# Pages turned later, square root's table loaded early, constants queued behind the first weights, and the input copied by VectorE, in a two-layer decoder step

## The chip, the cores and the metric

One NeuronCore of a Trainium2 chip runs the whole program in one launch. The metric is device time in microseconds (us), the median of three runs. TensorE (PE) multiplies and transposes, VectorE (DVE) and ScalarE (ACT) work elementwise, GpSimd (POOL) and SyncE (SP) issue DMAs, each engine in the order of its own program. They meet through semaphores.

## What is computed

The reference is one inference step of a two-layer decoder with D_MODEL 1024, on 512 prompt tokens and 8 x 4 sample tokens (544 columns in all). Layer 0 is retention and a gating MLP, with one joint input and one joint output projection. Layer 1 is sparse attention with three branches. Each layer ends with a gated convolution MLP, and every sub-layer stands between two RMS norms:

```python
def rms_norm(x, g):
    y = x * lax.rsqrt(jnp.mean(x * x, -1, keepdims=True) + EPS)
    return y * g
...
y = jnp.concatenate([ret_out, sg_out], axis=-1) @ w_out      # even layer's output projection
xp = xp + rms_norm(mp, norm_mix_post[l])
fp, cp = conv_ffn(rms_norm(xp, norm_ffn_pre[l]), ...)
xp = xp + rms_norm(fp, norm_ffn_post[l])
...
full_c = jnp.concatenate([gather_pages(pool_c, page_table), rows_c], axis=1)
kc, vc = compress(full_c, pe_k, pe_v, phi_k, phi_v)          # layer 1, from 16 cached pages
```

The compressed keys and values of the cached pages need nothing of layer 0, so the kernel makes them during layer 0.

## The kernel before

Activations lie transposed in SBUF: `xT` is 8 blocks (`dc`, `k` or `m`) of 128 features by 544 columns. Every matrix product is made of three products with operands split into a rounded high part and a rest: `hH` and `hL` for activations, `wH` and `wL` for weights.

**Weights** come in 107 units of up to 1 MB. SP loads a unit into one of two slots of `raw` (L505), as soon as the unit two before it has been split. ACT rounds it to `wH` (`split_hi`, L1158 is the line of every ACT operation), and DVE makes `wL` (`split_lo`, L1504). PE waits for that (`unit(u)`). The products go to one of two PSUM slots (`gemm`), by chunks of 128 output features: L582 and L849 for feature chunks, L598 for token chunks.

**A norm** squares the 8 blocks (ACT), sums them in PE (`square_sum`, L611, four matmuls after each square), takes the root (`root`, ACT Sqrt into `rq`), the reciprocal (`rec`, DVE L1510 into `rr`), spreads it over the partitions (`spread_rstd`, PE L618) and multiplies (DVE, `y`, L1522 before a sub-layer, L1532 and L1536 after it). `norm_fill` then makes `hH` (ACT) and `hL` (DVE L1515) block by block, 8 times. A function that is not in ACT's loaded table makes the compiler put a table load in front of it. `Copy`, `Square` and `Identity` never had one.

**The start.** SP issues the identity, the sample input, the prompt input in two DMAs of 1 MB (L500), then the weights. POOL issues `spread` and the four rows of gains (L1934), directly behind them 15 tables of constants for layer 0 (L1944) and two loads of the retention state (L1947). PE transposes the input block by block into two PSUM banks in turn (L557). For each block ACT copies the bank to `xT` and squares it. PE takes the square sum of block `dc - 1` behind the transposes of block `dc`. A bank is used again when its copy is done (`xt_ready`). DVE copies only the sample columns (L1540) and the gains (L1542), then runs `split_lo(0)` and behind it `norm_fill(0)`, which begins with the reciprocal.

**The output projection of layer 0** (`project_out(E_OUT)`, four units of two chunks, k0 to k7) carries the cached pages. I call the two pages of sample b pair p0 to p7. POOL looks up and loads 16 pages of 256 KB (`load_page`, L1970) after the barrier that ends the mixer (`meet`). Each page buffer holds four pages, so a page `n >= 4` waits until `pairs` of two pairs before has been filled. DVE rearranges a pair with two copies (L1721, semaphore `paired`), behind `split_lo` of the unit it stands with: p0 and p1 with the first, and so on. PE transposes it (`turn_pages`, L557, four transposes a page, two PSUM banks) in front of chunks k1 to k7, p7 behind k7. ACT takes each page out with two copies (`take_pages`, `page_ev`). In ACT's program they stand in front of that chunk's own copy, behind `split_hi` of the next unit where the chunk is the first of its unit. Page n is transposed when page n - 2 was taken out.

SP's loads of the phi weights (1 MB in four DMAs) and of the last output unit also start at that barrier. The other roots stand after this projection (`root(1)`), before and after both MLPs (`root(2)` to `root(4)`, `root(6)`, `root(7)`) and after layer 1's output projection (`root(5)`).

## Time and profile before

| | |
|---|---|
| three runs | 1733.72, 1735.07 and 1737.88 us; median 1735.07 us |
| the profiled execution | 1738.51 us, of which 1736.5 us from the first to the last instruction |
| mean granted TensorE clock | 0.952 |
| busy: PE, DVE, ACT, POOL | 92%, 45%, 40%, 13% of the span |
| instructions | 31072 |

All times of the trace count from the first instruction. In a timeline row the columns are start, duration, engine, line, operation, output and input by the program's names, and in brackets the idle time of the engine before it and what ended it. A row xN merges N instructions. In the chain of waits a row says from when, for how long and by what the end of the program was held up. "DMA" there is a transfer that is waited for. PEclk is the granted clock, 1.00 for 2.4 GHz and 0.50 for 1.2 GHz.

### The profile page before, as it was taken

The numbers are of one execution on the slowest core, as the hardware profiler recorded it, in microseconds if no ns is written. First come the engines' busy times: TensorE is split into PE (matmuls) and PEld (weight loads), VectorE is DVE, ScalarE is ACT, GpSimd is POOL, SyncE is SP. The second block draws the span as 40 slices with busy tenths as digits, with TensorE's granted clock in tenths as the row PEclk, the third lists the DMA queues.
The fourth block names the chain that finished last, engine by engine and source line by source line (L and its number), as shares of the span: only waits on it lengthen the run. The fifth ranks groups of instructions, "written<-read, shape, count | busy, mean of one in ns | idle before, by whom it ended". The sixth has DMA issues, their size and how long they took to land.

```text
span 1736.5 us, 31072 instructions
## 1 busy us (share of the span) xinstructions
PE 1603.8 (92%) x12951; PEld 1459.8 (84%) x12951; DVE 780.4 (45%) x1266; ACT 691.7 (40%) x1316; POOL 218.7 (13%) x582
## 2 busy tenths in 40 slices
PE   4999997999999999978999799988969999999996
PEld 2989976789999999967899556556859999999995
DVE  2565452455542555344112465653145553255523
ACT  4123123455542545223322465554335553255422
POOL 3000001200010000001013244432100000000000
PEclk8999998999999999987999898998979999999998
DMA  6122316312333232324333100004312223333231
GB/s 209 49 75 95 100 55 140 90 50 72 89 88 106 73 89 65 97 81 135 117 123 73 43 21 2 1 10 138 82 27 72 74 82 89 93 94 83 66 88 52
DMA packets 185559, 138.46 MB, mean 80 GB/s; under 512 B 11376, under 2 KB 177504, under 8 KB 185392
## 3 DMA queue, kind: packets, MB, share of 16 engines
q1 hardware_dynamic: 175536, 106.31, 21.5%
q0 software_dynamic: 9920, 30.74, 6.1%
q8 instruction: 69, 1.13, 0.3%
q14 instruction: 34, 0.28, 0.0%
HBM read 128.21 MB, written 13.01 MB: 81 GB/s over the span
## 4 chain that ended last, share of the span: by engine, by line
PE 79%; DVE 8%; ACT 5%; DMA 3%; issue 3%; POOLq 1%; POOL 1%; SPq 0%; DVEq 0%; ACTq 0%
PE gemm L849 40%; PE gemm L582 18%; PE gemm L598 9%; PE misc L557 5%; DMA raw<-in_o_w_in 2%; PE gemm L983 2%; PE misc L1014 1%; DVE y L1522 1%; DVE hL L1515 1%; ACT pr L1158 1%; DVE y L1532 1%; DVE pr L1812 1%; POOLq L490 1%; DVE xT L1536 1%; PE misc L618 1%
## 5 line engine op out<-in xcount | busy, mean ns | idle before, releaser
L1504 DVE TENSOR_TENSOR wL<-raw,wH 128x2048 fp32r<-128x2048 f32 (+2 forms) x107 | 222.1, 2075 | 256.3 <-ACT wH L1158 256.3
L849 PE MATMUL gemm<-hH,wH 128*128 128x272 f32 x1280 | 268.4, 291 | 0.0
L849 PE MATMUL gemm<-hH,wL 128*128 128x272 f32 x1280 | 264.9, 288 | 0.0
L849 PE MATMUL gemm<-hL,wH 128*128 128x272 f32 x1280 | 263.9, 288 | 0.0
L1158 ACT ACTIVATE wH<-raw 128x2048 fp32r<-128x2048 f32 (+2 forms) x107 | 185.3, 1732 | 64.1 <-PE gemm L582 32.7
L849 PEld LDWEIGHTS gemm<-hH,wH 128*128 128x128 f32 x1280 | 200.6, 188 | 5.9 <-issue 4.9
L849 PEld LDWEIGHTS gemm<-hL,wH 128*128 128x128 f32 x1280 | 201.1, 189 | 0.0
L849 PEld LDWEIGHTS gemm<-hH,wL 128*128 128x128 f32 x1280 | 199.8, 189 | 0.0
L598 PE MATMUL gemm<-wH,hH 128*128 128x256 f32 x560 | 164.8, 294 | 14.3 <-DVE hL L1515 8.5
L1732 DVE SCALAR_TENSOR_TENSOR conv<-up,rows_t,conv 128x560 f32<-128x560 f32 x88 | 70.5, 802 | 214.3 <-ACT conv L1158 214.3
L598 PE MATMUL gemm<-wL,hH 128*128 128x256 f32 x560 | 162.4, 290 | 0.0
L598 PE MATMUL gemm<-wH,hL 128*128 128x256 f32 x560 | 161.1, 288 | 0.0
L582 PE MATMUL gemm<-hH,wH 128*128 128x272 f32 (+1 forms) x656 | 141.8, 298 | 8.1 <-DVE hL L1515 4.5
L582 PE MATMUL gemm<-hL,wH 128*128 128x272 f32 (+1 forms) x656 | 137.8, 292 | 0.0
L582 PE MATMUL gemm<-hH,wL 128*128 128x272 f32 (+1 forms) x656 | 137.5, 291 | 0.0
L1158 ACT ACTIVATE up<-gemm 128x32 f32<-128x32 f32 (+2 forms) x264 | 66.0, 324 | 176.0 <-PE gemm L849 154.5
L598 PEld LDWEIGHTS gemm<-wH,hH 128*128 128x128 f32 x560 | 109.2, 195 | 19.4 <-DVE hL L1515 7.2
L582 PEld LDWEIGHTS gemm<-hH,wH 128*128 128x128 f32 (+1 forms) x656 | 104.4, 191 | 14.8 <-issue 9.0
L598 PEld LDWEIGHTS gemm<-wH,hL 128*128 128x128 f32 x560 | 110.3, 197 | 0.0
L849 PE MATMUL gemm<-aH,wH 128*128 128x272 f32 x528 | 110.2, 290 | 0.0
L598 PEld LDWEIGHTS gemm<-wL,hH 128*128 128x128 f32 x560 | 109.7, 196 | 0.0
L849 PE MATMUL gemm<-aH,wL 128*128 128x272 f32 x528 | 108.9, 287 | 0.0
(329 smaller groups left out, 2672.9 us busy)
## 6 DMA issues: line engine op xcount, KB each, us to landing
raw<-in_f_w_in SPq DMA_DIRECT2D x88, 512.0 KB, 5.0
raw<-in_f_w_out SPq DMA_DIRECT2D x32, 704.0 KB, 4.6
raw<-in_e_w_in SPq DMA_DIRECT2D x12, 1024.0 KB, 5.1
raw<-in_o_w_in SPq DMA_DIRECT2D x10, 1024.0 KB, 5.2
raw<-in_e_w_out SPq DMA_DIRECT2D x4, 1024.0 KB, 6.7
pages<-in_cache_cmp POOLq DMA_DIRECT2D x16, 256.0 KB, 3.5
raw<-in_o_w_out SPq DMA_DIRECT2D x16, 256.0 KB, 6.1
rows<-in_cache_sel POOLq DMA_DIRECT2D x12, 256.0 KB, 2.9
```

What stands on the lines that cost most here:

```text
L490: page = eng.value_load(a["page_table"][b:b + 1, pg:pg + 1], min_val=0, max_val=N_POOL - 1)
L557: ins = pe.transpose(out, in_, ident[base:base + k, base:base + k])
L582: ins = pe.matmul(gemm[c % 2][0:m, n, 0:TH], w, x[:, k, n * TH:(n + 1) * TH], start=(n_k == 0 and part == 0), stop=(n_k == nk - 1 and part ...
L598: ins = pe.matmul(gemm[c % 2][:, 0, 0:width], x, w, start=(k == 0 and part == 0), stop=(k == DC - 1 and part == 2))
L618: ins = pe.matmul(misc[:, 1 + q // 2, (q % 2) * TQ:(q % 2 + 1) * TQ], spread[:, q, :], rr[:, :], start=True, stop=True)
L849: ins = pe.matmul(gemm[odd][:, n, 0:TH], w, x[:, k, n * TH:(n + 1) * TH], start=(k == 0 and part == 0), stop=(k == nk - 1 and part == 2))
L983: ins = pe.matmul(slot[:, g2, 0:keys], qTs[j][half, r, rows], (ksT, kwT)[br][half, j, 0:keys], start=True, stop=True)
L1014: ins = pe.matmul(misc[64 * g2:64 * g2 + 64, 2 + grp % 2, r * P:(r + 1) * P], kvN[:, 1 + kt, (2 * br + 3) * 256 + g * HD:(2 * br + 3) * 25 ...
L1158: order(act.activation(out, in_, func, **kw), sem_)
L1504: order(dve.tensor_tensor(unit_view(wL, u), unit_view(raw, u), unit_view(wH, u).bitcast(F32), ALU.subtract), lo_ready)
L1515: order(dve.tensor_tensor(hL[:, k, :], src, hH[:, k, :].bitcast(F32), ALU.subtract), h_ready)
L1732: order(dve.scalar_tensor_tensor(conv[:, j, :], U[:, j, 1:1 + CW], w[:, 17:18], conv[:, j, :], ALU.mult, ALU.add))
```

## The change

Five edits in one:

1. `turn_pages` and `take_pages` follow a table `PAGES_AT`: p0 in front of k3, p1 of k4, p2 of k5, p3 and p4 of k6, p5 and p6 of k7, p7 still behind k7. DVE's rearrangement follows `PAIRED_AT`: none with the first unit, p0 and p1 with the second, p2 to p4 with the third, p5 to p7 with the fourth.
2. `load_root` is a Sqrt of a 128x1 tile into a tile that nothing reads. It stands at ACT's very start, in front of the squares of retention's norm, in layer 1's output projection behind the second unit's `split_hi`, and in each MLP behind the first output chunk of its second half.
3. POOL waits for the first weight unit to land before it issues the 15 constants and what follows.
4. DVE instead of ACT copies the 8 input blocks out of PSUM.
5. In the first norm DVE does the reciprocal first and `split_lo(0)` behind it.

```diff
--- before.py
+++ after.py
@@ -209,6 +209,7 @@
         spread = sb("spread_sb", [P, 4, P])
         mean_d, mean_k = sb("mean_d", [P, 32]), sb("mean_k", [P, 32])
         eps, pool_mark = sb("eps", [P, 1]), sb("pool_mark", [1, 1])
+        root_probe = sb("root_probe", [P, 1])
         gains = sb("gains", [P, DC, 8])
         kcs = sb("kcs", [P, DB, 2, NCS])
         vcs = sb("vcs", [2 * NCS, DB, P])
@@ -411,6 +412,8 @@
             if eng is nc.gpsimd:
                 eng.wait_ge(phase, N_BAR * (n + 1))
 
+        PAGES_AT = {3: (0,), 4: (1,), 5: (2,), 6: (3, 4), 7: (5, 6)}
+        PAIRED_AT = ((), (0, 1), (2, 3, 4), (5, 6, 7))
         FILL_AFTER = [0, E_OUT, F0, O_IN, F1]
         NORM_GAIN = [0, 2, 4, 6, 1, 3, 5, 7]
 
@@ -810,8 +813,9 @@
                 for i in range(4):
                     unit(first + i)
                     for j in range(2):
-                        if fill and 2 * i + j:
-                            turn_pages(4 * i + 2 * j - 2)
+                        if fill:
+                            for b in PAGES_AT.get(2 * i + j, ()):
+                                turn_pages(2 * b)
                         feature_chunk(first + i, j, DC, hH, hL, fill if i == j == 0 else None, MIX_FIRST,
                                       part_of=(4 if fill and i == j == 0 else 0, None))
                         if 2 * i + j:
@@ -1193,14 +1197,16 @@
                 act.wait_ge(gemm_done, c + 1)
                 return gemm[c % 2]
 
+            def load_root():
+
+                activate(root_probe[:, :], eps[:, 0:1], ACT.Sqrt)
+
+            act.wait_ge(consts, 3)
+            load_root()
+            act.wait_ge(gain_ready, 1)
             for dc in range(DC):
-                act.wait_ge(xt_turned, dc + 2)
-                activate(xT[:, dc, NS:T], misc[:, 1 + 2 * (dc % 2), :], ACT.Copy, xt_ready)
-                if dc == 0:
-                    act.wait_ge(gain_ready, 1)
                 act.wait_ge(xt_ready, dc + 1)
                 square(0, dc, xT[:, dc, :], sqx)
-            act.wait_ge(gain_ready, 2)
             root(0)
 
             split_hi(0)
@@ -1228,6 +1234,7 @@
                             activate(lns[:, 2, :], lns[:, 1, :], ACT.Sqrt, ln_root, bias=eps[:, 0:1], scale=1.0 / P)
                     elif what in (6, 7):
                         activate(halves(silu_g[:, 2 * (what - 6) + j, :]), chunk_ready(c)[:, :, 0:TH], ACT.Silu, evacuated[c % 2])
+            load_root()
             act.wait_ge(o_ev, 4)
             act.wait_ge(so_ev, 4)
             for h in range(RH):
@@ -1269,9 +1276,12 @@
             def project_out(first, n):
                 for i in range(4):
                     split_hi(first + i + 1)
+                    if first == O_OUT and i == 0:
+                        load_root()
                     for j in range(2):
-                        if first == E_OUT and 2 * i + j:
-                            take_pages(4 * i + 2 * j - 2)
+                        if first == E_OUT:
+                            for b in PAGES_AT.get(2 * i + j, ()):
+                                take_pages(2 * b)
                         c, m = FIRST_CHUNK[first + i] + j, 2 * i + j
                         activate(halves(y[:, m, :]), chunk_ready(c)[:, :, 0:TH], ACT.Copy, evacuated[c % 2])
                         act.wait_ge(evacuated[c % 2], c // 2 + 1)
@@ -1339,6 +1349,8 @@
                             square(n, m, y[:, m, :], sqf)
                         if m == 0:
                             tail_out(e, FH - 1, half, layer)
+                            if half:
+                                load_root()
                 root(n)
 
             def tail_out(e, i, half, layer):
@@ -1516,7 +1528,13 @@
 
             def norm_fill(n, fill):
 
-                rec(n)
+                if n:
+                    rec(n)
+                else:
+                    dve.wait_ge(root_ready, 1)
+                    order(dve.reciprocal(rr[:, :], rq[:, :]), rec_ready)
+                    split_lo(0)
+                    dve.wait_ge(rstd_ready, 1)
                 for k in range(DC + 1):
                     if k < DC:
                         order(dve.scalar_tensor_tensor(halves(y[:, k, :]), halves(xT[:, k, :]), gains[:, k, NORM_GAIN[n]:NORM_GAIN[n] + 1],
@@ -1538,9 +1556,12 @@
 
             dve.wait_ge(xt_turned, 1)
             order(dve.tensor_copy(xT[:, :, 0:NS], misc[:, 2, 0:DC * NS].rearrange("p (c t) -> p c t", c=DC)), gain_ready)
+            for dc in range(DC):
+                dve.wait_ge(xt_turned, dc + 2)
+                order(dve.tensor_copy(xT[:, dc, NS:T], misc[:, 1 + 2 * (dc % 2), :]), xt_ready)
             dve.wait_ge(xt_turned, DC + 2)
             order(dve.tensor_copy(gains[:, :, :], gemm[1][:, 0, 0:DC * 8].rearrange("p (c t) -> p c t", c=DC)), gain_ready)
-            split_lo(0)
+            order.wait()
             norm_fill(0, 0)
             meet(dve, order, 0)
 
@@ -1712,7 +1733,7 @@
                         for z in range(2):
                             order(dve.memset(cT[:, z, :, :, 2 * DB, :], 0.0), pe_clear)
                     if first == E_OUT:
-                        for b in (2 * i, 2 * i + 1):
+                        for b in PAIRED_AT[i]:
                             for n in (2 * b, 2 * b + 1):
                                 dve.wait_ge(page_in[n % 4], 16 * (n // 4 + 1))
                             if b >= 2:
@@ -1934,6 +1955,7 @@
                 pool.dma_start(dst, src).then_inc(loads, 16)
             order(pool.memset(pool_mark[:, :], 0.0), phase)
 
+            pool.wait_ge(raw_ready[0], landed[0])
             for dst, src in ((decay[:, :, :], by4(a["decay"])), (decs[:, :, :], by4(a["decay_s"])),
                              (qdec[:, :, :], by4(a["qdecay"].to_broadcast([P, 4 * P]))), (qdecs[:, :, :], by4(a["qdecay_s"].to_broadcast([P, 4 * NS]))),
                              (kdec[:, :], a["kdecay"]), (batch_of[:, :], a["batch_of"]), (same_s[:, :], a["same_s"]), (row_of_s[:, :], a["row_of_s"]),
```

## Rows read from the trace of the kernel before

**Rows 1.** Page, part 4: the chain that ended last, by engine.

```profile
PE 79%; DVE 8%; ACT 5%; DMA 3%; issue 3%; POOLq 1%; POOL 1%; SPq 0%; DVEq 0%; ACTq 0%
```

**Rows 2.** Chain of waits, 0 to 48 us: start, us, what.

```profile
2.27 11.14 DMA xin<-in_x_prompt
...
27.11 1.28 ACT L1158
...
28.78 1.81 ACT wH L1158
...
30.61 2.29 DVE wL L1504
...
33.87 2.20 PE misc L618 x8
...
36.09 0.79 DVE y L1522
```

**Rows 3.** Timeline of ACT, one copy of an input block.

```profile
22.82 0.60 ACT L1158 ACTIVATE xT<-misc 128x512 f32<-128x512 f32 x1
```

**Rows 4.** Timeline of DVE, end of layer 0's mixer.

```profile
223.89 0.69 DVE L1614 COPY qT<-misc 128x512 f32<-128x512 f32 x1 [6.58 <-PE misc L669]
...
250.88 2.62 DVE L1515 TENSOR_TENSOR hL<-uT,hH 128x544 fp32r<-128x544 f32 x4
253.62 3.55 DVE L1697 RECIPROCAL kT<-kT 128x544 f32<-128x544 f32 x1
```

**Rows 5.** DMA, 0 to 13.4 us: POOL's queue; state loads, us to landing.

```profile
q0 software_dynamic: 572, 0.95, 26.2%
...
s<-in_state_ret POOLq DMA_DIRECT2D x2, 512.0 KB, 14.6
```

**Rows 6.** DMA, 2.7 to 3.19 us: the first weight unit.

```profile
raw<-in_e_w_in SPq DMA_DIRECT2D x1, 1024.0 KB, 22.3
```

**Rows 7.** Windows: busy PE, PEld, DVE, ACT, POOL; PEclk, DMA, GB/s.

```profile
28.00:30.00 2.00, 0.00 (x0) 0.00 (x0) 0.00 (x0) 1.99 (x3) 0.00 (x0) 0.50 0.08 27
50.00:52.00 2.00, 2.00 (x14) 2.00 (x13) 1.01 (x2) 0.00 (x0) 0.00 (x0) 0.68 0.11 17
```

**Rows 8.** Timeline of PE, the first pages of layer 0's output projection.

```profile
277.08 1.97 PE L557 MATMUL misc<-ident_sb,pairs 128*128 128x128 f32 x8 [11.88 <-DVE pairs L1721]
```

**Rows 9.** Chain of waits, layer 0's output projection.

```profile
279.05 6.46 PE gemm L582 x48
285.51 0.37 PE misc L611 x8
285.88 1.02 PE misc L557 x8
286.91 6.02 PE gemm L582 x48
```

**Rows 10.** Timeline of ACT behind chunk k5, in front of k6.

```profile
315.16 0.62 ACT L1158 ACTIVATE y<-gemm 128x544 f32<-128x544 f32 x1 [4.99 <-PE gemm L582]
...
318.18 1.18 ACT L1158 ACTIVATE cT<-misc 128x256 f32<-128x256 f32 x4
```

**Rows 11.** Pages: all 16 landings; then timelines of DVE and of POOL.

```profile
DMA to landing us min/median/max: 3.3/3.5/7.5
...
290.91 1.55 DVE L1721 COPY pairs<-pages 128x512 f32<-128x512 f32 x4
...
295.66 0.51 POOL L1970 DMA_DIRECT2D pages<-in_cache_cmp  x1 [6.98 <-issue]
298.43 0.51 POOL L1970 DMA_DIRECT2D pages<-in_cache_cmp  x1 [2.25 <-issue]
```

**Rows 12.** Timeline of ACT, first MLP's end.

```profile
766.89 0.66 ACT L1158 ACTIVATE conv<-y 128x544 f32<-128x544 f32 x1 [6.36 <-DVE y L1753]
767.56 1.28 ACT L1158 ACT_TABLE_LOAD   x1
768.86 0.37 ACT L1158 ACTIVATE rq<-misc,eps 128x136 f32<-128x136 f32 x1
```

## The prediction, made before the changed kernel was built

> **What bounds the kernel now.** I read the chain that ended last first: PE holds 79% of it, DVE 8%, ACT 5%, DMA 3% [rows 1]. So outside PE's products only the stretches in which PE waits for another engine can give time. I then went through the chain and the timelines at the places that the change touches, and kept three kinds.
>
> First the start. The end of the program hangs on the second half of the prompt input until 13.41, then on eight rounds of transpose, copy, square and sum, then on a chain that nothing overlaps: table load, root, rounding of the first weights on ACT, their rest on DVE, reciprocal, spread on PE, and the first scaled block at 36.09 [rows 2].
>
> Second the output projection of layer 0. PE sits idle for 11.88 us behind k0, for the first page pair [rows 8]. Behind that wait everything is PE again: sum 0.37, a pair 1.02, a chunk 6.02 [rows 9].
>
> Third the roots. Behind the last square of a norm ACT loads the table for 1.28 us, then takes the root at once [rows 12]. Of this form there are three: at 767.56, 1276.43 and 1711.26. The load at 27.11 differs: it began only when PE's last sum was done [rows 2]. A fourth load stands in front of the root of the retention norm [rows 4].
>
> **The input (constants held back).** By 13.4 us POOL's queue had taken 26.2% of the 16 engines' time, 3.5 us, for 0.95 MB [rows 5]. Of this, `spread` and the gains are 0.29 MB and stay. The other 0.66 MB are constants, in proportion 0.66/0.95 x 3.5 = 2.4 us. Some of them are tiny packets, which take more time than their bytes, so I take 2.5 us: the input lands at about 10.9. The bounds are 0 (they filled gaps only) and 3.5 (all of the queue's time). What is held: POOL waits for the first weight unit. Behind that wait stand the 15 constants, the two state loads, and much later POOL's stores. That unit landed at 2.8 + 22.3 = 25.1 [rows 6] because the queues shared. Alone behind 2.3 MB of input it lands near 13. The slowest of the held loads took 14.6 us [rows 5], so even issued up to 22 us they land before 40, and their first reader (layer norm) comes behind two weight units, after 70 us. Cost nothing. Cover gone only if they landed 30 us later.
>
> **The copies on DVE.** An ACT copy of a block is 0.60 us [rows 3]. DVE's nearest row, a copy of 512 columns out of PSUM, is 0.69 [rows 4]. ACT no longer alternates, but the period does not come from ACT alone. A PSUM bank is used again two blocks later, and PE places the sum (which waits for the square) in front of that transpose. So copy, square, sum and transpose form a loop over two blocks, and DVE's 0.09 us adds 0.045 a block: 6 x 0.045 for the loop and 0.09 on the last copy, about +0.3 us. The bounds are -0.3 (PE slow at first, which hides it, and ACT free earlier) and +0.7 (all eight in series). DVE has nothing else there. The gains copy stands behind, and is off the chain.
>
> **The first root and the new order.** The table load at 27.11 goes to ACT's start, where ACT waits for the input anyway: -1.28. The probe that loads it is a 128x1 operation in that same wait. Next, DVE now takes the reciprocal before the first `wL`. Before: rounding from 28.78, `wL` 30.61 to 32.90, then reciprocal, spread from 33.87 to 36.07, block at 36.09 [rows 2]. Now the reciprocal (about 1 us) and the spread (2.20 us, still at the slow rate) run beside rounding. In times of before less 1.28, rounding ends at 29.3, `wL` runs 29.3 to 31.6, the spread ends by 30.8. So `wL` is what is late next, and the block starts at 31.65 instead of 36.09: -4.44 in all, of which -3.16 is the order. It needs the first weights by 25 us, which the held constants secure. Start: -2.5 + 0.3 - 4.44 = -6.6 us.
>
> **The pages.** In times of before, k0 ends at 277.08 - 11.88 = 265.2 on PE [rows 8]. Gone are the idle 11.88 us and the slow clock behind it (1.97 against 1.02 for the pair, 6.46 against 6.02 for the chunk) [rows 8, 9]: 13.3 us. What can come in its place, chunk by chunk. k1 runs to 271.2, sum and k2 to 277.6, sum to 278.0. DVE makes `wL` of the third unit from about 274.4 to 276.6, and p0 behind it (0.8 us for a pair, by 1.55 for two [rows 11]) by 277.4. Its pages had landed by 276.2, as PE took the pair at 277.08 [rows 8]. So k3 does not wait, with 0.6 us to spare. p1 is wanted at 285.4; two pages at 2.8 us each behind p0's [rows 11] make it ready near 282.6. Loads of the MLP's first weights now start at about 277 instead of 291 and may hold it by 2 us, which is covered. p2, at 291.2, is wanted at 292.8. The new thing is two pairs in front of k6 and k7. In front of k6 ACT copies k5, squares, rounds a whole unit and only then takes pages out: the first page of p3 begins to leave 3.02 us behind k5's end (318.18 against 315.16 [rows 10]). PE has p3 in both banks 1.4 us behind k5's end and needs a bank at 3.6 and the next at 4.2. k6 then starts 4.8 us behind k5 instead of 0.37 + 2 x 1.02 = 2.4: a stall of 2.4. In front of k7 there is no rounding, and the same sequence costs about 0.6. Are pages there? p4 loads when p2 is rearranged: 291.2, 3.9 us to the first issue, 2.8 to the second, 3.5 landing (291.7 to 295.66 and 298.43, median landing [rows 11]), copies 0.8, so 302.2, before ACT is ready at 303.6. p6, loaded behind p4, comes at about 312.5 and is wanted at 312. All in all 3.0 us of stalls, and k7 ends at 319.7 instead of 330.0: -10.3. Bounds: -13.3 (no stall) and -5 (p1, p4 and p6 each some 2.5 us late). `split_lo` of the fourth unit now stands behind p1 on DVE, and that of the next behind p4. Their readers are k6 and the MLP 30 us later.
>
> The Trainium skill ("SBUF — State Buffer", section "SBUF: two separate sides") says that a DMA issued by GpSimd cannot get its descriptors written while VectorE runs a float32 copy within SBUF. That speaks against bunching six such copies: they are 0.39 us each here, so it would hold a page by at most 2.3 us, and the landings of 3.3 to 3.5 us show no such hold while the copies came in fours [rows 11].
>
> **The three roots.** Without the load the root has to wait for PE's sum: square ends at 767.55, sum 0.37 us and two hops make 768.07, against 768.86 [rows 9, 12]. So 0.79 comes back and not 1.28, three times: -2.4. Where the loads went: behind `split_hi` in `project_out(O_OUT)`, where ACT idles 7 us, and behind the first output chunk of each MLP's second half, where the next `wH` is 1.5 us later and PE wants it 2.6 us later still. Nothing. The retention root: `hL` ends at 250.88 + 2.62 = 253.50 on DVE, and the reciprocal behind it began at 253.62 [rows 4]. -0.1.
>
> The Trainium skill ("ScalarE: Activation LUTs", section "What ACT_TABLE_LOAD costs") puts a drain of about 1.38 us beside each load, 2.66 in all. By that figure the sum would be some 5.5 us larger. The trace does not agree: 767.55, 767.56, 768.84, 768.86 leave no room for a drain [rows 12].
>
> **Sum.** -6.6 - 10.3 - 2.4 - 0.1 = -19.4 us on the profiled execution of 1738.5 us, thus 1719.1. That execution lies 3.4 us above the median of the runs. The same loss from 1735.07 gives **1715.7**.
>
> **Rivals.**
> (A) *Pages still set the pace* in a milder form: p1, p4 or p6 late by 4 to 6 us together, since weights and pages share the DMA. For it: one page took 7.5 us [rows 11]. Against: it stood beside the phi weights. About 1720.7.
> (B) *The clock stays up at the start.* It was at half in 28 to 30 and rose in 50 to 52 [rows 7]. PE's idle stretch behind the last sum shrinks from 6.8 to 1.5 us. If it stays full to the dense products (46.3 to 51.2 before), these take half: another -2.4, 1713.3. Against: PE is still mostly idle in the eight blocks between.
> (C) *The input lands no earlier*, because its own queue and not the shared engines set it: 2.5 lost, 1718.2.
> (D) *The early loads do nothing*, because the compiler places a load in front of the root anyway: 1.28 + 2.4 + 0.1 lost, 1719.5. Against: roots that follow a root had no load.
> (E) *Slower: the reload of the page buffers.* p4 waits for p2's buffer, p6 for p4's. If a page takes 14.6 us to land, like the state loads beside a full queue [rows 5], one such step is 3.9 + 2.8 + 14.6 + 0.8 = 22.1, so p4 comes at 313.3, p6 at 335.4, k7 ends at 342.4, 12.4 later than before, with two more slow starts of 1.4: +15.2 - 9.1 = +6.1, 1741.2. It turns into a loss from a landing of about 11.5 us. Against: 3.5 is the median.
>
> **How the numbers follow.** Chances: forecast 0.58, A 0.15, B 0.11, C 0.07, D 0.05, E 0.04. The likeliest is 1715.7. The range takes in A to D, on the low side B with no stall at all (1710.3) and 3 us for the clock's phase and the median's own spread (the runs lie 4 us apart), on the high side A with part of C: 1707 to 1724. A measurement tells about 0.2%, 3.5 us, from no change. All but E are faster by more, less a little for A, C and D together: 0.95, 0.02, 0.03.
>
> **What would show it.** Input landed by 11, the first `y` at 29 to 30, no table load behind the first one until Silu's. PE's idle stretch in front of the first pair gone, k3 without a wait, a stall of about 2.4 in front of k6 whose releaser is ACT (`page_ev`) and not DVE. Roots 0.5 us behind the last square. The prediction is wrong if pages release PE in front of k4 or k6, if the input lands after 12, or if time is lost in a stage that the change does not touch.

## The result, and the profile after

The changed kernel takes 1715.7 us (median, 1711.65 to 1716.69) where the kernel before, beside it, took 1736.5 (1733.72 to 1741.87). Repeated with more runs it takes 1714.8 us, a ratio of 0.9861 with a 95% interval of 0.9842 to 0.9879. The predicted time is met. The saving isn't: the sum said 19.4 us, a ratio of 0.9888, which lies outside the interval, and the measured ratio is worth about 24 us (21 to 28 by the interval). The three runs from which I subtracted lay at the lower end of what the kernel before takes: its medians beside this run and beside the experiments were 1736.5 to 1740.5. So there are about 5 us to account for that no step names.

The page of the changed kernel, its parts 1, 2 and 4 (span 1710.0 us of 1711.65; before: 1736.5 of 1738.51, the chain in [rows 1]):

```profile
PE 1595.6 (93%) x12951; PEld 1453.0 (85%) x12951; DVE 785.8 (46%) x1274; ACT 687.2 (40%) x1312; POOL 219.1 (13%) x582
...
PEclk8999999999999999987999899999979999999998
...
PE 66%; DVE 6%; ACT 3%; issue 2%; DMA 2%; POOLq 1%; POOL 1%; DVEq 0%; ACTq 0%
```

PE's busy share is up by one point and its mean granted clock is 0.964 instead of 0.952. The chain isn't to be compared with the 79% of PE in [rows 1]: its shares add up to 81% only, since followed back it ends at 298.9 us, in POOL's lookup of a page number, and the time in front of that isn't in it. Lines have moved: ACT's L1158 is L1162 now, the pages' L557 is L560, L1721 is L1742, L1970 is L1992.

**The start.** Timeline of ACT, DVE and PE in the changed kernel, against [rows 2 to 4]:

```profile
0.88 1.28 ACT L1162 ACT_TABLE_LOAD   x1 [0.88 <-PEq L2162]
2.17 0.20 ACT L1162 ACTIVATE root_probe<-eps 128x1 f32<-128x1 f32 x1
11.26 0.95 PE L560 MATMUL misc<-ident_sb,xin 32*128 32x32 f32 x7 [11.26 <-DMA xin<-in_x_prompt]
25.39 0.38 ACT L1162 ACTIVATE rq<-misc,eps 128x136 f32<-128x136 f32 x1 [0.56 <-PE misc L614]
25.66 1.90 ACT L1162 ACTIVATE wH<-raw 128x2048 fp32r<-128x2048 f32 x1
25.87 1.00 DVE L1535 RECIPROCAL rr<-rq 128x136 f32<-128x136 f32 x1 [0.67 <-ACT rq L1162]
26.93 2.18 PE L621 MATMUL misc<-rr,spread_sb 128*128 128x136 f32 x8 [1.61 <-DVE rr L1535]
27.59 2.29 DVE L1516 TENSOR_TENSOR wL<-raw,wH 128x2048 fp32r<-128x2048 f32 x1 [0.72 <-ACT wH L1162]
29.80 1.47 DVE L1540 SCALAR_TENSOR_TENSOR y<-xT,gains,misc 128x544 f32<-128x544 f32 x2
```

The table load now ends long before the input lands. The reciprocal and the spread (26.93 to 29.11) lie beside the rounding and `wL`, and `y` starts as `wL` ends, where before it started 3.2 us behind the end of `wL` (32.90 and 36.09, [rows 2]): `wL` is what is late, as predicted.

**The pages.** All pairs in front of k3 to k7, on PE, against [rows 8, 9]:

```profile
269.87 1.09 PE L560 MATMUL misc<-ident_sb,pairs 128*128 128x128 f32 x8
277.27 1.09 PE L560 MATMUL misc<-ident_sb,pairs 128*128 128x128 f32 x8
284.68 1.09 PE L560 MATMUL misc<-ident_sb,pairs 128*128 128x128 f32 x8
292.10 1.09 PE L560 MATMUL misc<-ident_sb,pairs 128*128 128x128 f32 x8
295.64 1.41 PE L560 MATMUL misc<-ident_sb,pairs 128*128 128x128 f32 x8 [2.45 <-ACT cT L1162]
304.62 1.10 PE L560 MATMUL misc<-ident_sb,pairs 128*128 128x128 f32 x8
307.15 1.09 PE L560 MATMUL misc<-ident_sb,pairs 128*128 128x128 f32 x8 [1.44 <-DVE pairs L1742]
```

The 11.88 us are gone, and k3, k4 and k5 wait for nothing. Two waits are new: 2.45 us in front of k6, released by ACT, and 1.44 in front of k7, released by DVE. ACT at the first of them, against [rows 10]:

```profile
291.83 0.63 ACT L1162 ACTIVATE y<-gemm 128x544 f32<-128x544 f32 x1 [5.01 <-PE gemm L585]
292.49 0.66 ACT L1162 ACTIVATE sqm<-y 128x544 f32<-128x544 f32 x1
293.06 1.89 ACT L1162 ACTIVATE wH<-raw 128x2048 fp32r<-128x2048 f32 x1
294.86 1.19 ACT L1162 ACTIVATE cT<-misc 128x256 f32<-128x256 f32 x4
```

The first page begins to leave 3.03 us behind the end of k5, because a whole unit is rounded first. The pair behind the wait takes 1.41 us instead of 1.09. In the windows of the changed kernel (columns as in [rows 7]) the clock is low there, and a second time in the residual stage behind this projection:

```profile
298.00:300.00 2.00, 2.00 (x11) 2.00 (x11) 0.76 (x2) 0.00 (x0) 0.51 (x1) 0.57 0.59 174
300.00:304.00 4.00, 4.00 (x34) 4.00 (x33) 0.00 (x0) 0.00 (x0) 0.51 (x1) 1.00 1.10 252
...
323.00:327.00 4.00, 3.70 (x30) 1.42 (x28) 4.00 (x7) 1.95 (x4) 0.41 (x1) 0.58 0.12 32
```

**The roots.** End of the first MLP, against [rows 12]. No load, and the root waits for PE's sum:

```profile
752.51 0.66 ACT L1162 ACTIVATE conv<-y 128x544 f32<-128x544 f32 x1 [6.41 <-DVE y L1774]
753.72 0.37 ACT L1162 ACTIVATE rq<-misc,eps 128x136 f32<-128x136 f32 x1 [0.56 <-PE misc L614]
```

**Where the time went**, from the timelines of both profiled executions (start of the operation named, us):

| | before | after | gained by then |
|---|---|---|---|
| input on PE | 13.45 | 11.26 | 2.2 |
| root of the first norm | 28.40 | 25.39 | 3.0 |
| first `y` | 36.09 | 29.80 | 6.3 |
| second unit of the output projection rounded | 263.55 | 255.32 | 8.2 |
| k7 ends | 329.96 | 314.27 | 15.7 |
| root before the first MLP | 347.48 | 332.63 | 14.9 |
| root behind the first MLP | 768.86 | 753.72 | 15.1 |
| fourth unit of layer 1's input projection rounded | 832.23 | 815.24 | 17.0 |
| its seventh unit rounded | 877.51 | 859.05 | 18.5 |
| table of Exp (attention begins) | 973.43 | 953.74 | 19.7 |
| second unit of layer 1's output projection rounded, attention over | 1220.63 | 1196.38 | 24.3 |
| root behind the last MLP | 1712.56 | 1686.88 | 25.7 |

Up to the root behind the first MLP the gain is 15.1 us, where the sum has 17.8 (all but two of the roots). Then 10.6 us appear behind it, of which the two roots explain 1.5. Attention alone (from the load of Exp's table to the rounding of that unit) took 242 to 247 us in the profiled executions of all kernels, with no order by edit, so its 4.6 us here are spread. What layer 1's input projection gained is not: it comes back below.

### The profile page after: what moved, and what is told of

Its sections match the earlier page's. It is cut to its first block, busy times and chain, and to the rows that moved or that the text cites. A ratio compares the mean times of both kernels' runs of the same rounds, so it can differ in the third digit from the quotient of the medians.

```text
span 1710.0 us, 31077 instructions
## 1 busy us (share of the span) xinstructions
PE 1595.6 (93%) x12951; PEld 1453.0 (85%) x12951; DVE 785.8 (46%) x1274; ACT 687.2 (40%) x1312; POOL 219.1 (13%) x582
## 4 chain that ended last, share of the span: by engine, by line
PE 66%; DVE 6%; ACT 3%; issue 2%; DMA 2%; POOLq 1%; POOL 1%; DVEq 0%; ACTq 0%
PE gemm L853 40%; PE gemm L585 10%; PE gemm L601 6%; PE misc L560 4%; DMA raw<-in_o_w_in 2%; PE gemm L987 2%; PE misc L1018 1%; DVE y L1550 1%; ACT pr L1162 1%; DVE pr L1833 1%; DVE y L1540 1%; DVE xT L1554 1%; POOLq L493 1%; DVE hL L1527 1%; PE misc L621 1%
## 5 line engine op out<-in xcount | busy, mean ns | idle before, releaser
L1162 ACT ACTIVATE wH<-raw 128x2048 fp32r<-128x2048 f32 (+2 forms) x107 | 185.2, 1731 | 61.1 <-PE gemm L585 32.7
L1162 ACT ACTIVATE up<-gemm 128x32 f32<-128x32 f32 (+2 forms) x264 | 66.0, 324 | 176.0 <-PE gemm L853 154.5
L601 PEld LDWEIGHTS gemm<-wH,hH 128*128 128x128 f32 x560 | 108.3, 193 | 17.8 <-DVE hL L1527 7.2
L853 PE MATMUL gemm<-aL,wH 128*128 128x272 f32 x528 | 109.1, 288 | 0.0
```

The costliest lines, as they stand in the source:

```text
L601: ins = pe.matmul(gemm[c % 2][:, 0, 0:width], x, w, start=(k == 0 and part == 0), stop=(k == DC - 1 and part == 2))
L853: ins = pe.matmul(gemm[odd][:, n, 0:TH], w, x[:, k, n * TH:(n + 1) * TH], start=(k == 0 and part == 0), stop=(k == nk - 1 and part == 2))
L1162: order(act.activation(out, in_, func, **kw), sem_)
```

## The experiments

My theory at first: each gain stands where the sum puts it, and what layer 1 shows is either spread or an effect of a step. The rivals were that the pages or the early tables act at a distance (another phase of the clock, other collisions of transfers), and a thing in the diff that I had put at nothing: `root_probe` is a tile of 128x1, and everything allocated behind it, from `gains` on, lies 32 bytes further in SBUF.

### The two kernels again, the pages alone, all but the pages

```diff
# pages_only: the kernel before, with edit 1 alone
+        PAGES_AT = {3: (0,), 4: (1,), 5: (2,), 6: (3, 4), 7: (5, 6)}
+        PAIRED_AT = ((), (0, 1), (2, 3, 4), (5, 6, 7))
...
# no_pages: the changed kernel, edit 1 undone
-                        for b in PAIRED_AT[i]:
+                        for b in (2 * i, 2 * i + 1):
```

> The changed kernel once more, unchanged. In its first profile it was 26.5 us shorter than before, of which 8.9 us came about between the sixth unit of layer 1's input projection and the end of its attention, where the change touches nothing. My theory: those 8.9 us are the spread of that stage from run to run, so a second profile keeps -6.3 us at the first scaled block, about -15 us behind layer 0's output projection and -0.7 us at each of three roots, while the attention's share comes out between 0 and -9. Ratio to before 0.9885 (about -20 us). Rival: the earlier start shifts layer 1 against its DMAs for good, then the 8.9 us come again and the ratio is 0.985.

> The kernel before once more, for the spread of its own stages. My theory: outside the attention of layer 1 every stage ends within 1.5 us of the first profile, and the attention (from the input projection's end to the output projection's start, 288.3 us in the first profile of before against 282.6 in the changed kernel) differs by several us from the first one. Rival: it repeats within 1 us, and then the attention's gain belongs to the change. Ratio 1.000.

> The kernel before with edit 1 alone: pages turned and rearranged later. The changed kernel gained 7.5 us between the end of k0 and the end of k7, and gave 0.85 us back in the stage behind it, where PE's clock fell. If that is the edit itself, this kernel does the same: k0's end to k7's end 57.3 us instead of 64.8, with a wait of some 2.5 us in front of k6 ended by ACT, 1.4 us in front of k7 ended by DVE, and the slow clock once behind k6's wait. Total -7 us, ratio 0.996. By my prediction (stalls of 3.0 us in all, no slow clock) it would be 54.5 us. Rival: the clock's fall depends on where its stretches happen to lie, and this kernel, 8 us later in time, shows none: 56 us.

> The changed kernel with edit 1 undone, all else kept. If the edits add up, PE again idles about 11.9 us behind k0 and the total is 7 us longer than the changed kernel: ratio to before 0.9925. Rival (interaction): with the mixer 8 us earlier the page loads meet another DMA load, and the idle time is not 11.9 but 10 or 14 us.

Ratios to the kernel before: 0.9861 [0.9842, 0.9879] for the changed kernel again, 1.0003 [0.9991, 1.0016] for the kernel before against itself, 0.9946 [0.9926, 0.9965] for the pages alone, 0.9908 [0.989, 0.9926] for all but the pages. So the pages are worth 9.4 us one way and 8.2 the other, within the bounds of 5 and 13.3 and under the 10.3 forecast.

Three of these four expectations missed. The kernel before again was not within 1.5 us of itself outside the attention: from the end of k0 to that of k7 it took 66.9 us instead of 64.8, and from the second to the seventh unit of layer 1's input projection 82.5 instead of 79.6. The changed kernel again came out at 0.9861, between the 0.9885 of the theory and the 0.985 of its rival; from the second unit of that projection to the end of the attention it took 416.3 us, where the first profiles have 422.7 and 413.6 and the kernel before again 423.8. So most of that gain came again; the tile, below, is part of it. The pages alone took 60.1 us from k0 to k7 and not 57.3, because two pairs came late. Their timeline has the two waits again, here with a late first pair:

```profile
278.98 1.09 PE L559 MATMUL misc<-ident_sb,pairs 128*128 128x128 f32 x8 [1.50 <-DVE pairs L1725]
...
304.74 1.11 PE L559 MATMUL misc<-ident_sb,pairs 128*128 128x128 f32 x8 [2.44 <-ACT cT L1161]
...
315.98 1.09 PE L559 MATMUL misc<-ident_sb,pairs 128*128 128x128 f32 x8 [2.72 <-DVE pairs L1725]
```

ACT's wait is 2.44 or 2.45 us in all eight kernels that have this edit and ACT's rounding in its old place. The ones that DVE releases vary: 0 to 1.50 in front of k3, 1.44 to 2.98 in front of k7. So does the slow clock. In seven of the eight it follows ACT's wait. In the pages alone it doesn't (the second pair takes 1.11 us) and comes behind the 2.72 us in front of k7, as the windows of that kernel show:

```profile
306.00:310.00 4.00, 4.00 (x34) 4.00 (x34) 1.15 (x3) 0.62 (x3) 0.51 (x1) 1.00 0.71 211
...
317.00:320.00 3.00, 3.00 (x16) 3.00 (x15) 0.00 (x0) 0.89 (x4) 0.51 (x1) 0.52 0.29 87
```

And without the pages' edit the old wait is back in full:

```profile
271.92 1.97 PE L560 MATMUL misc<-ident_sb,pairs 128*128 128x128 f32 x8 [12.77 <-DVE pairs L1740]
```

How much it is differs from kernel to kernel: 11.88 us in the profile from which I forecast, about 12.6 in the kernel before again, 14.0 in pad_only (below). The stretch from ACT's rounding of the projection's second unit to the root behind k7 took 68.9, 71.0, 71.1 and 71.7 us in the four kernels without edit 1, the first being that profile, and 61.4 to 64.5 in the seven that have it and nothing else changed in this stage. The means are 70.7 and 62.6. Their difference, 8.1 us, agrees with the ratios.

### The tile alone

```diff
# pad_only: the kernel before, with a tile that nothing uses
         eps, pool_mark = sb("eps", [P, 1]), sb("pool_mark", [1, 1])
+        root_probe = sb("root_probe", [P, 1])
         gains = sb("gains", [P, DC, 8])
```

> The kernel before with nothing but the new 128x1 tile allocated (no instruction uses it), which moves every later tile in SBUF by 32 bytes. In both profiles of the changed kernel and in the one without edit 1 the third unit of layer 1's input projection lands 28.2 to 28.8 us after its issue, in the kernels without that tile (before twice, edit 1 alone) after 30.0 to 31.4 us. Theory: the tile's shift does that (the DMAs beside it write to shifted addresses): then 28.2 to 28.9 here, total -2 us, ratio 0.999. Rival: it is the stage's timing against the clock or the DMA queues, then 30.0 to 31.5 and ratio 1.000.

0.9971 [0.9951, 0.999]: an unused tile of four bytes a partition takes 5.0 us off the kernel (1.7 to 8.5 by the interval, 2 expected). No instruction differs. The kernel's own `sb` rounds a tile up to 32 bytes a partition, so everything allocated behind it moves by 32. Chain of waits in layer 1, the kernel before and then the one with the tile:

```profile
802.16 30.05 DMA raw<-in_o_w_in
```

```profile
805.10 28.32 DMA raw<-in_o_w_in
```

It is the fourth unit of layer 1's input projection (the expectations count it as the third), and the program waits for it there in every kernel. While it loads, the DMA engines also carry the first store of new cache rows, the phi weights and a copy of the window's state. `raw` lies in front of the new tile and didn't move. `kvN`, from which rows are stored, and the phi weights did. The page's part on DMA shows it at the small stores (KB each, us to landing) and at POOL's queue (share of 16 engines), the kernel before and then the one with the tile:

```profile
q0 software_dynamic: 9920, 30.74, 6.1%
...
out_win_sample<-kvN POOLq DMA_DIRECT2D x8, 8.0 KB, 3.1
```

```profile
q0 software_dynamic: 9920, 30.74, 5.7%
...
out_win_sample<-kvN POOLq DMA_DIRECT2D x8, 8.0 KB, 2.8
```

The same packets and bytes take less of the engines' time.

### A second tile

If it is the place in SBUF, a second such tile, which shifts everything by 64 bytes instead of 32, should take the gain back. If it is any other layout, or chance, it should not.

```diff
         root_probe = sb("root_probe", [P, 1])
+        spare = sb("spare", [P, 1])
         gains = sb("gains", [P, DC, 8])
```

> The changed kernel with a second unused tile of 128x1 in front of gains, so that everything behind it lies 64 bytes further than in the kernel before instead of 32. Theory (the 32 bytes put the input and weight buffers where the transfers land faster): the third unit of layer 1's input projection lands 30.0 to 31.4 us after its issue, as in the kernels without the tile, not 28.2 to 29.4; the program takes 3 to 5 us more than the changed kernel, a ratio near 0.989 to the kernel before. Rival (any other layout, or chance): the landing stays at 28.2 to 29.4 us and the ratio at 0.986.

0.9883 [0.9855, 0.9911], 3.8 us above the changed kernel's ratio. The two intervals overlap, so the ratio alone would not settle it. Measured beside the same runs of the kernel before, this kernel took 1720.1 us and three others with one tile (act_copies, ids_take and doubles, below) 1712.3 to 1714.7. The stage settles it (landing of that unit, POOL's queue, small stores):

```profile
789.38 31.56 DMA raw<-in_o_w_in
```

```profile
q0 software_dynamic: 9920, 30.74, 6.2%
...
out_win_sample<-kvN POOLq DMA_DIRECT2D x8, 8.0 KB, 3.1
```

Over all 14 profiled executions, by where the tiles behind `eps` lie:

| shift of those tiles | kernels | `kvN` small stores | landing of that unit | second to seventh unit of that projection (us from ACT's rounding of the one to that of the other) |
|---|---|---|---|---|
| 0 bytes | before, before_again, pages_only | 3.1 | 30.05, 31.43, 30.83 | 79.6, 82.5, 81.9 |
| 64 bytes | two_tiles | 3.1 | 31.56 | 82.7 |
| 32 bytes | the ten others | 2.8 to 2.9 | 28.19 to 29.60 | 76.3 to 79.2, mean 77.2 |

No kernel crosses over, though the last column's two groups nearly touch (79.2 and 79.6). The difference of the means, 81.7 against 77.2, is 4.5 us, and pad_only as a whole gave 5.0. Which of the moved tiles it is wasn't tried, nor any other shift.

(My expectation for this run named the weight buffers among what moved. They didn't; that what is loaded there gains by sharing the engines is my reading, and no run separates it.)

### The constants, the early tables, the copies

```diff
# no_hold: the changed kernel without edit 3
-            pool.wait_ge(raw_ready[0], landed[0])
# no_roots: the changed kernel without the four load_root() calls
-            load_root()
# act_copies: the changed kernel without edit 4 (DVE's loop of copies is taken out as well)
+                act.wait_ge(xt_turned, dc + 2)
+                activate(xT[:, dc, NS:T], misc[:, 1 + 2 * (dc % 2), :], ACT.Copy, xt_ready)
```

> The changed kernel without edit 3: the constants are issued at once again. Theory: the prompt input lands at 13.4 instead of 11.2 us and nothing else is late, since the first weights are there at about 25 us and are wanted at 27.5: first scaled block at 31.9 instead of 29.7, +2.2 us. Rival: with the root's table already loaded the first weights have become the bound, and the block comes at 32.5 or later; or, the other way, the input lands no later and all is as in the changed kernel.

> The changed kernel without edit 2: no early loads of the root's table. Theory: +1.28 us at the first block (31.0 us), +0.1 at the retention root, +0.75 behind each of the three roots of the MLPs and of layer 1's output projection, as the two profiles of the changed kernel gained 0.7 to 0.76 there: +3.6 us, ratio to before 0.988. Rival from the price with a drain (2.66 us a load): +2.7 at the first block and +2.1 at each of the three, +9 us.

> The changed kernel without edit 4: ScalarE copies the input again, as in the kernel before. Theory (VectorE's copies of the input cost more than ScalarE's, with its squares and sums in one queue): the input lands at 11.2 us all the same, the first y comes 0.3 to 0.5 us earlier, at 29.3 us, and the total doesn't tell it from the changed kernel. Rival (ScalarE was in the way): the first y 0.3 us later or more, at 30.0 us.

Without the hold: 0.9882 [0.985, 0.9915]. The input is on PE at 12.76 instead of 11.26, and the first `y` at 31.18 instead of 29.80:

```profile
12.76 1.46 PE L560 MATMUL misc<-ident_sb,xin 32*128 32x32 f32 x9 [12.76 <-DMA xin<-in_x_prompt]
```

So the hold is worth 1.5 us of landing, not 2.5, and 1.4 at the first `y`, not the 2.2 expected of this run. The total lost 3.7 us by the ratios, with intervals that also allow 1.4. The kernel before had 13.45 (13.23 again, 13.25 with the tile alone, 13.85 with the pages alone). The 0.5 us or more by which 12.76 is earlier came with neither this edit nor the tile nor any other that I can name.

Without the early tables: 0.9885 [0.9858, 0.9912], about 4 us by the ratio. The load is back in front of each of the roots:

```profile
13.66 1.28 ACT L1162 ACT_TABLE_LOAD   x1 [13.66 <-DVE xT L1555]
14.95 1.20 ACT L1162 ACTIVATE sqx<-xT 128x544 f32<-128x544 f32 x2
...
25.48 1.28 ACT L1162 ACT_TABLE_LOAD   x1
26.78 0.37 ACT L1162 ACTIVATE rq<-misc,eps 128x136 f32<-128x136 f32 x1
...
755.87 0.66 ACT L1162 ACTIVATE conv<-y 128x544 f32<-128x544 f32 x1 [6.36 <-DVE y L1768]
756.54 1.28 ACT L1162 ACT_TABLE_LOAD   x1
757.84 0.37 ACT L1162 ACTIVATE rq<-misc,eps 128x136 f32<-128x136 f32 x1
```

The first `y` comes 1.39 us later, but that doesn't confirm the forecast of 1.28. This kernel has a second change at the start. The program's first table load stood at 0.88 in every other kernel, in front of ACT's first operation. Here that operation is the first square, so the load waits for the input and begins at 13.66, on the chain. (Of `Square` I had written that it never had a load.) The squares begin 0.76 us later than in the changed kernel, although the input is on PE at 10.72 instead of 11.26. The load in front of the root begins at 25.48, before PE's last sum ends at 25.96, and the root comes 0.82 us behind that sum instead of 0.07: it costs 0.75 us here. In the kernel before it began only at 27.11, behind the sum, and the root came 1.40 behind that. The diff also deletes ACT's wait for the gains in front of this root, which may be the reason; that wasn't tried. The 1.28 rests on the two profiles, before and after (1.40 to 0.07).

From the last rounding in front of the first MLP's last root to that root it is 10.22 or 10.23 us in all five kernels with the load there, and 9.46 to 9.52 in the nine without: 0.75. Measured in the same way, it is 0.76 behind layer 1's output projection and 0.75 behind the last MLP. The forecast had three times 0.79. The Trainium skill ("ScalarE: Activation LUTs", section "What ACT_TABLE_LOAD costs") gives 2.66 us for a load with its drain. The rows agree with its 1.28 for the load alone. A load on the chain, taken away and put back, moved the root by 0.75 where PE's sum came next, and no row shows the drain.

With ACT's copies back: 0.9859 [0.9821, 0.9896], 1714.67 us, not told apart from the changed kernel. The input is on PE at 11.18, the root comes at 24.93 instead of 25.39 and `y` at 29.34 instead of 29.80:

```profile
24.93 0.37 ACT L1162 ACTIVATE rq<-misc,eps 128x136 f32<-128x136 f32 x1 [0.56 <-PE misc L614]
```

Edit 4 therefore costs 0.4 to 0.5 us (forecast 0.3) and gives nothing back.

### Page numbers early, and the rounding behind the pages

The late pair in front of k7 is released by DVE, but DVE waits for the pages, and these for POOL. Its timeline in the changed kernel:

```profile
298.36 0.51 POOL L1992 DMA_DIRECT2D pages<-in_cache_cmp  x1 [2.26 <-issue]
302.51 0.51 POOL L1992 DMA_DIRECT2D pages<-in_cache_cmp  x1 [3.63 <-issue]
```

Where POOL waits for no buffer, 2.0 to 2.3 us lie between two issues, in which it only reads the next page's number. The second page of p6 took 3.63, and the pair with it was late. That is no accident: the same page took 3.6 to 4.2 us in all seven kernels with edit 1 that look it up there. It falls on SP's loads of the MLP's first weights, issued from 297.44. From 298.9 to 302.4 us the page's part on DMA has for their queue (packets, MB, share of 16 engines)

```profile
q1 hardware_dynamic: 1820, 0.92, 95.2%
```

and 21.4% during the next lookup, which took 2.23. That the read waits for these transfers is the likely reading, but only argued. One kernel reads the 16 numbers early, behind the constants. The next also lets ACT round the last unit behind its work on the pages, and so tests what the wait in front of k6 is made of.

```diff
# ids_early
+            numbers = [pool.value_load(...) for n in range(DB * NPG)]
...
-                page = pool.value_load(...)
+                page = numbers[n]
# ids_take: that, and in ACT's project_out
+                    late = first == E_OUT and i == 3
+                    if not late:
+                        split_hi(first + i + 1)
...
+                        if late and j == 0:
+                            split_hi(first + i + 1)
```

> The changed kernel with the 16 page numbers read into registers at the start of POOL's program, where it is idle, instead of one by one in front of each page's DMA (2.0 us of the 2.7 us between two issues). Theory: pages are what ends the wait in front of k7 (1.44 us, by DVE's rearrangement of p6), and ACT's unit rounding what ends the 2.45 us in front of k6. Then the wait in front of k7 falls to 0.6 us or less, the one in front of k6 stays at 2.4 with its slow clock behind it, and k7 ends 1.0 us earlier, counted from k0. Rival: both waits are the pages', then both go and k7 ends 3.5 to 5 us earlier.

> The changed kernel with the sixteen page numbers read into registers at GpSimd's start, and with ScalarE rounding the last weight unit only behind its work on the pages in front of k6. Theory (ScalarE's rounding of a unit is what the pages in front of k6 wait for, and the slow clock behind that wait is its second price): the wait in front of k6 falls from 2.44 to about 0.6 us, no stretch of clock 0.50 behind it, and from the last but one first-half product's unit to the root of layer 0's residual 57.5 us instead of 60.6; ratio 0.984. Rival (the last unit is then itself late): the wait comes back in front of k7 at 2 us or more and the total stays at 0.986.

With early numbers: 0.9854 [0.9828, 0.9879]. Four pages are now issued within 2.31 us. In front of k7 only 0.64 is left, and the releaser is ACT. In front of k6 it is 2.44 as before, and the pair behind it takes 1.57 us. With the rounding moved, 1712.3 us and 0.9837 [0.9801, 0.9874]:

```profile
295.29 1.11 PE L560 MATMUL misc<-ident_sb,pairs 128*128 128x128 f32 x8 [0.65 <-ACT cT L1162]
...
304.47 1.11 PE L560 MATMUL misc<-ident_sb,pairs 128*128 128x128 f32 x8 [0.65 <-ACT cT L1162]
```

The wait is 1.79 us shorter, the second pair takes 1.11 and k6 is over at the full clock. From the rounding of the projection's second unit to the root behind k7 (the stretch of the expectations) the stage took 61.4 us in the changed kernel, 60.6 with early numbers and 57.3 here (57.5 expected). Of the last 3.3 us, 1.8 are the wait and most of the rest is the slow clock that followed it. So in front of k6 it is ACT's rounding, as forecast, and what it cost was nearly double the wait that it made.

### The pages in five groups

This kernel too has the page numbers early, and no pair behind k7:

```diff
-        PAGES_AT = {3: (0,), 4: (1,), 5: (2,), 6: (3, 4), 7: (5, 6)}
-        PAIRED_AT = ((), (0, 1), (2, 3, 4), (5, 6, 7))
+        PAGES_AT = {3: (0, 1), 4: (2,), 5: (3, 4), 6: (5,), 7: (6, 7)}
+        PAIRED_AT = ((0, 1), (2, 3), (4, 5), (6, 7))
```

> The changed kernel with the page numbers in registers at GpSimd's start and the pages turned in groups at k3, k4, k5, k6 and k7, with no pair left behind k7. Theory (what the pages cost in this stage is their places and what ScalarE and VectorE still do there): waits of about 0.6 us each in front of k3, k5 and k7, no pair of pages at the end of the stage, the same stretch as above at 56 to 57 us; total 4 us under the changed kernel, ratio 0.983. Rival (the work of the pages only moves to where VectorE is the later one): waits of over 2 us in front of one of the chunks, the stretch at 60 us or more, ratio 0.986.

1713.1 us, 0.9845 [0.9815, 0.9875]. The double pairs stand where ACT rounds nothing, and wait little:

```profile
273.98 1.11 PE L560 MATMUL misc<-ident_sb,pairs 128*128 128x128 f32 x8 [0.65 <-ACT cT L1160]
...
290.57 1.11 PE L560 MATMUL misc<-ident_sb,pairs 128*128 128x128 f32 x8 [0.65 <-ACT cT L1160]
...
307.15 1.11 PE L560 MATMUL misc<-ident_sb,pairs 128*128 128x128 f32 x8 [0.42 <-ACT cT L1160]
```

The stage took 58.5 us where 56 to 57 were expected, and the ratio was to be 0.983. p7 in front of k7 costs its own 1.1 us and the wait of 0.42. Behind k7 it had hidden in part: the root came 2.5 us behind the end of k7 with it, and comes 1.9 behind it without.

Both versions lie about 0.2% below the changed kernel. The intervals overlap with its own, so the totals don't prove them better. The stage shows them 2.9 to 4.1 us shorter.

## Why the prediction was right, point by point

- **Idle stretch in front of the first pair, k3 to k5 free of waits: right.** The bank order, ACT's 3.02 us [rows 10] and the stall of 2.4 in front of k6 came as worked out (3.03 and 2.45), with ACT as the releaser, and ids_take shows the rounding as its cause. Rival A is in the trace in a small form: p6 is what k7 waits for, 1.4 to 3.0 us where the forecast had 0.6.
- **The pages' size: 10.3 forecast, 7.5 in the two profiles** (from the end of k0 to that of k7, 64.8 against 57.3), 8.1 between the means of all kernels, 8.2 and 9.4 by ratio. Three terms make up nearly all of the 2.8. "k7 ends at 319.7" has k6 at the full rate. It took 7.2 us instead of 6.02 at the half clock behind the wait. I had priced this for the old stall [rows 8, 9] and not for the new one. k7 began 4.0 us behind k6 instead of 3.0, by the slow lookup of one page number beside the MLP's weights. The forecast let those weights hold p1 and not p6. And k6 began some 0.4 us later than counted. On the other side the profile that I started from had the shortest wait and the shortest stage of the four without this edit, 2 to 3 us under the others.
- **The residual stage: not in the sum.** It took 0.8 us longer than before, with a stretch at half clock at 323 to 327. But it took 15.1 to 16.0 us in the kernels with and without edit 1, and my first profile was among the shortest, so this is spread. So are the 1.9 us gained in the mixer, which no edit touches: from the first `y` to the rounding of the second output unit the 14 profiles took 225.4 to 228.0 us, in no order by edit, and the kernel before again had 225.7. By the mean granted clock, PE was at the half clock for about 167 us before (171 again) and for 123 after (123 again), with 142 to 149 in the kernels that have the tile alone, the pages alone or all but the pages. I can't tell which edit moved which stretch.
- **The start: 6.6 forecast, 6.3 measured.** Landing 2.2 (forecast 2.5), copies +0.5 (+0.3, confirmed by act_copies), table and order 4.6 (4.44). The first of these is right in size only: the held constants gave 1.5 of the 2.2. The order has no run of its own; it is read from the timelines. Between the means of the kernels with all of these edits and those with none the first `y` gained 6.8.
- **The roots: 3 x 0.79 forecast, 0.75 or 0.76 at three places.** Rival D, that the compiler would load anyway, is out. So are B (the clock was at 0.50 still at 30 to 32 us), C (the input came 2.2 us earlier) and E (the pages landed in 3.1 to 6.8 us).
- **The hold cost nothing, as said.** The first weights were there when ACT came for them at 25.66.
- **What failed: "if time is lost in a stage that the change does not touch".** I had thought of losses only, and put the tile of the probe at nothing ("The probe that loads it is a 128x1 operation in that same wait"). Its operation costs nothing. Its place in SBUF gives 5.0 us, most of it in layer 1's input projection (4.5 between the means). That is the part of the gain that the sum lacks: 6.8 for the start, 8.1 for the pages, 2.3 for the roots and 4.5 for the tile make 21.7 us, within the 21 to 28 of the measured ratio. In the predicted time it was offset by two things that I had no right to: pages that gave about 2 us less, and a median of before that lay low.

So the mechanisms were right, but that the time came out exact is luck. Three errors cancelled: the pages gave 1 to 2 us less, the tile gave 5 that nobody foresaw, and the base lay up to 5 us low.

## What to carry over

Before pricing a reordering, list every new or grown tile in the diff and what lies behind it in SBUF: a shift of 32 bytes was worth 5.0 us here, as much as the early tables or the constants' hold. Test such a thing with an unused tile alone. Profile the kernel before twice before you price a stage from it: its own stages differed by 2 to 3 us. When an edit is taken out for a test, look at what else moves with it: without the early tables the program's first load fell onto the chain. Price a stall of PE with the slow clock that can follow it (behind 2.45 us of wait the next chunk lost 1.2 us), and look at who is busy on the releasing engine just before: moving one rounding behind the pages took most of it away.

## What the runs showed of the hardware

- Tiles moved by 32 bytes in SBUF: small stores out of `kvN` land in 2.8 us instead of 3.1, POOL's queue takes 5.7 to 6.0% of the engines instead of 6.1 to 6.2% for the same packets, a contended weight unit lands in 28.2 to 29.6 instead of 30.1 to 31.6, and 64 bytes undo it. That unit's own buffer wasn't moved.
- Reading one page number on POOL takes 2.0 to 2.3 us before each load, and 3.6 to 4.2 where the weights' queue took 77 to 95% of the DMA engines. Read early, they left the issues less than 0.6 us apart.
- A wait of 2.44 or 2.45 us between chunks was followed by a stretch at half clock in seven kernels of eight, and so were waits of 2.72 and 2.98. Waits of 0.4 to 1.9 us in this stage were not.
- A table load right behind the last square delays a root by 0.75 us, and not by its own 1.28, where PE's sum was still under way.
